# Behind the convolution in halves, and the last block of the pooling mixer split first

## What the reference computes

```python
def conformer_conv(h, w1, b1, w_dw, b_dw, ln_g, ln_b, w2, b2):      # mixer of layer 0
    u = h @ w1 + b1
    a, gate = split(u, 2)
    u = a * sigmoid(gate)
    u = depthwise causal conv of width 31 over the tokens + b_dw
    u = silu(layernorm(u, ln_g, ln_b))
    return u @ w2 + b2

def pool_mixer(h, w_grp, b_grp, scale):                             # mixer of layer 1
    for 4 groups of 256 features, windows 2, 4, 8, 16:
        p[g] = trailing mean of h[g] over the window - h[g]
    return (p[g] @ w_grp[g] + b_grp[g]) * scale

def sqrelu_mlp(h, w1, w2):                                          # behind either mixer
    return relu(h @ w1) ** 2 @ w2                                   # 1024 -> 4096 -> 1024
```

## Time and profile before

| | |
|---|---|
| time, median of 3 runs (lowest to highest) | 902.92 us (902.45 to 903.51) |
| the profiled execution: time | 903.05 us |
| its span, first to last instruction | 901.1 us |
| mean granted clock of TensorE | 0.997 of full |
| TensorE busy | 881.5 us, 98% of the span |
| VectorE busy | 704.9 us, 78% |
| ScalarE busy | 458.6 us, 51% |
| GpSimd busy | 149.1 us, 17% |

### The profile page before, as it was taken

One profiled execution on the slowest core, in us unless ns is written; L12 is line 12 of the kernel. 1 busy time (PEld: TensorE's weight loads), 2 busy tenths in 40 slices (PEclk: granted clock), 3 DMA queues, 4 the chain that ended last, 5 costly groups with the idle time before them and its releaser, 6 DMA issues.

```text
span 901.1 us, 11943 instructions
## 1 busy us (share of the span) xinstructions
PE 881.5 (98%) x4408; PEld 746.4 (83%) x4408; DVE 704.9 (78%) x946; ACT 458.6 (51%) x663; POOL 149.1 (17%) x128
## 2 busy tenths in 40 slices
PE   8999998999999999999999999999999999999996
PEld 8888876889888888888888888988888888888885
DVE  5799999867877778696868888687776868686856
ACT  5778686245462727354353645446262634435243
POOL 1499993270000020000000041000000000000000
PEclk9999999999999999999999999999999999999999
DMA  9614022205133131414224023113313142332102
GB/s 278 196 48 117 5 90 117 109 32 187 49 140 140 47 140 47 141 72 159 100 87 163 18 101 117 47 48 141 140 47 140 47 147 83 143 117 70 71 1 94
DMA packets 48376, 90.81 MB, mean 101 GB/s; under 512 B 1458, under 2 KB 18866, under 8 KB 48340
## 3 DMA queue, kind: packets, MB, share of 16 engines
q1 hardware_dynamic: 48340, 90.32, 29.2%
HBM read 88.22 MB, written 2.10 MB: 100 GB/s over the span
## 4 chain that ended last, share of the span: by engine, by line
PE 77%; DVE 8%; POOL 8%; DMA 2%; issue 2%; ACT 1%; SPq 0%; POOLq 0%; DVEq 0%; ACTq 0%
PE ps L1319 16%; PE ps L1321 16%; PE ps L1320 16%; PE ps L1520 10%; PE ps L1518 10%; PE ps L1519 10%; POOL w_lo L376 3%; POOL merged_a L386 3%; DMA w_raw<-in_conv_w 2%; POOL merged_b L386 2%; DVE ps L906 2%; PE ps L1338 1%; DVE tok L819 1%; DVE act_lo L825 1%; DVE bn L875 1%
## 5 line engine op out<-in xcount | busy, mean ns | idle before, releaser
L1319 PE MATMUL ps<-act_hi,w_hi 128*128 128x512 f32 (+1 forms) x712 | 262.2, 368 | 1.5 <-DVE act_lo L825 1.4
L1321 PE MATMUL ps<-act_hi,w_lo 128*128 128x512 f32 (+1 forms) x712 | 261.0, 367 | 0.0
L1320 PE MATMUL ps<-act_lo,w_hi 128*128 128x512 f32 (+1 forms) x712 | 261.0, 367 | 0.0
L1319 PEld LDWEIGHTS ps<-act_hi,w_hi 128*128 128x128 f32 x712 | 134.2, 189 | 23.8 <-DVE act_lo L825 2.0
L1520 PE MATMUL ps<-w_hi,u_lo 128*128 128x512 f32 x392 | 152.7, 390 | 0.0
L1518 PE MATMUL ps<-w_hi,u_hi 128*128 128x512 f32 x392 | 152.7, 389 | 0.0
L1321 PEld LDWEIGHTS ps<-act_hi,w_lo 128*128 128x128 f32 x712 | 134.2, 189 | 22.1
L1519 PE MATMUL ps<-w_lo,u_hi 128*128 128x512 f32 x392 | 152.5, 389 | 0.0
L1320 PEld LDWEIGHTS ps<-act_lo,w_hi 128*128 128x128 f32 x712 | 134.3, 189 | 21.8
L619 ACT ACTIVATE relu<-ps 128x512 f32<-128x512 f32 x36 | 21.5, 597 | 243.0 <-PE ps L1321 243.0
L1057 DVE TENSOR_TENSOR w_lo<-w_raw,w_hi 128x1024 fp32r<-128x1024 f32 x70 | 85.1, 1221 | 58.0 <-ACT w_hi L640 58.0
(11 more groups left out here) (206 smaller groups left out, 1274.8 us busy)
## 6 DMA issues: line engine op xcount, KB each, us to landing
w_raw<-in_mlp_w SPq DMA_DIRECT2D x32, 1024.0 KB, 5.0
w_raw<-in_mlp_w SPq DMA_DIRECT2D x16, 2048.0 KB, 8.1
w_raw<-in_conv_w SPq DMA_DIRECT2D x16, 512.0 KB, 5.9
w_raw<-in_conv_w SPq DMA_DIRECT2D x2, 2048.0 KB, 9.7
h<-in_x SPq DMA_DIRECT2D x4, 512.0 KB, 6.8
out<-tok SPq DMA_DIRECT2D x8, 256.0 KB, 2.3
gain<-in_norm_mix SPq DMA_DIRECT2D x2, 512.0 KB, 6.5
gain<-in_norm_mlp SPq DMA_DIRECT2D x2, 512.0 KB, 6.3
```

The lines of the kernel that those rows point to most:

```text
L1319: nc.tensor.matmul(dst, lh, rh, start=(n == 0), stop=False)
L1320: nc.tensor.matmul(dst, lh, rl, start=False, stop=False)
L1321: return nc.tensor.matmul(dst, ll, rh, start=False, stop=(n == count - 1))
```

## The change

Five parts:

1. In the last chunk of the convolution ScalarE takes 13 taps instead of 11, GpSimd 4 instead of 5, VectorE 14 instead of 15.
2. The statistics of the last chunk are read from PSUM bank 5; ScalarE copies it to `ctok` behind that read (`bn_read`).
3. Blocks 0 and 1 go through the norm in halves (with `center_half`, and half of block 2's), and the orders on VectorE and ScalarE are written anew; the four `c2b_low` stand behind the work on the blocks.
4. On TensorE the products of the rounded block (`out_high`) come ahead of those with the rest (`out_low`); each part waits for its half alone. 24 matmuls keep the clock instead of 28.
5. Pooling mixer: `proj_low(3)` stands ahead of `add_pool(2)`; `pool_band(3)` goes to banks 2 and 3 and does not wait for `add_pool(2)`; `add_pool(3)` stands behind `mlp_norm(2)`. The first MLP group of layer 1 uses banks 0, 1, 2, 3, starts with the rounded blocks, and turns blocks 2 and 3 behind j = 1 and j = 2.

```diff
-SHARE = (5, 5, 5, 5, 5, 5, 5, 11)
-POOL_LAST = 5
+SHARE = (5, 5, 5, 5, 5, 5, 5, 13)
+POOL_LAST = 4
...
 UP_BANK = (2, 3, 0, 1)
+FIRST_BANK = (UP_BANK, (0, 1, 2, 3))
...
         def pool_bank(b):
-            return 4 if b == 1 else 0
+            return (0, 4, 0, 2)[b]
...
             c2_high(3)
             nc.scalar.activation(stats[:, 3, 36:37], ident[:, 0:1], ACT.Sqrt)
+            act.wait_ge(bn_read, 1)
             ctok_copy(NC - 1)
...
-            c2b_high(0)
-            for b in range(1, NB):
-                if b >= 2:
-                    act_high(GEN_LN, b - 1)
+            def high_half(b, k):
+                if k == 0:
+                    act.wait_ge(turned_half, b + 1)
+                else:
+                    act.wait_ge(turned, 4 * GEN_LN + b + 1)
+                cs = slice(k * NC // 2, (k + 1) * NC // 2)
+                nc.scalar.copy(act_hi[:, cs, b * P:(b + 1) * P],
+                               turn_banks(GEN_LN, b)[:, cs]).then_inc(act_hi_ok if k else act_half_hi, 1)
+
+            def swish_sigmoid(b):
                 act.wait_ge(y_ok, b + 1)
                 act.wait_ge(tok_ok, 4 * GEN_LN + b)
                 nc.scalar.activation(spare, tok[:, b % 2, :], ACT.Sigmoid).then_inc(swish_sig, 1)
-                c2b_high(b)
-            act_high(GEN_LN, NB - 1)
+
+            high_half(0, 0)
+            act.wait_ge(y_ok, 1)
+            nc.scalar.activation(spare[:, high], tok[:, 0, high], ACT.Sigmoid).then_inc(swish_sig, 1)
+            high_half(0, 1)
+            swish_sigmoid(1)
+            act.wait_ge(w1_in, 16)
+            c2b_high(0)
+            high_half(1, 0)
+            high_half(1, 1)
+            swish_sigmoid(2)
+            c2b_high(1)
+            c2b_high(2)
+            act_high(GEN_LN, 2)
+            swish_sigmoid(3)
+            c2b_high(3)
+            act_high(GEN_LN, 3)
 
             def w1_high(layer, g, j):
...
             bn_part(1, 4, 7)
-            last = bn_part(2, 7, 8)
-            link(last)
+            dve.wait_ge(conv_turned, NC)
+            for b in range(NB):
+                last = nc.vector.bn_stats(bn[:, b, 2, :], ps[:, 4 + (NC - 1) % 2, b * P:(b + 1) * P])
+            last.then_inc(bn_read, 1)
+            dve.wait_ge(bn_read, 1)
             for b in range(NB):
                 last = nc.vector.bn_aggr(moments[:, b, :], bn[:, b].rearrange("p a k -> p (a k)"))
             link(last)
...
+            def center_half(b, k):
+                at = slice(k * 512, (k + 1) * 512)
+                link(nc.vector.scalar_tensor_tensor(tok[:, b % 2, at], ctok[:, b, at], moments[:, b, 0:1], gain[:, 0, at],
+                                                    ALU.subtract, ALU.mult))
...
+            def shift_half(b, k):
+                nc.vector.scalar_tensor_tensor(tok[:, b % 2, at], tok[:, b % 2, at], rinv[:, 32 + b:33 + b], gain[:, 1, at],
+                                               ALU.mult, ALU.add).then_inc(y_ok if k else y_half, 1)
...
+            def low_half(k):
+                if k == 0:
+                    dve.wait_ge(act_half_hi, 1)
+                else:
+                    dve.wait_ge(act_hi_ok, 4 * GEN_LN + 1)
+                cs = slice(k * NC // 2, (k + 1) * NC // 2)
+                nc.vector.tensor_tensor(act_lo[:, cs, 0:P], turn_banks(GEN_LN, 0)[:, cs], act_hi[:, cs, 0:P].bitcast(F32),
+                                        ALU.subtract).then_inc(act_lo_ok if k else act_half_lo, 1)
...
-            center(0)
+            dve.wait_ge(ctok_ok, NC)
+            center_half(0, 0)
...
+            shift_half(0, 0)
+            center_half(0, 1)
+            swish_half(0, 0)
+            shift_half(0, 1)
+            center(1)
+            swish_half(0, 1)
+            low_half(0)
             shift(1)
-            center(2)
-            swish(1)
+            dve.wait_ge(turned, 4 * GEN_LN + 1)
+            center_half(2, 0)
+            low_half(1)
+            swish_half(1, 0)
+            swish_half(1, 1)
+            center_half(2, 1)
             shift(2)
-            c2b_low(0)
+            dve.wait_ge(act_half_hi, 2)
             act_low(GEN_LN, 1)
+            swish(2)
             center(3)
-            swish(2)
             shift(3)
-            c2b_low(1)
             act_low(GEN_LN, 2)
             swish(3)
+            c2b_low(0)
+            act_low(GEN_LN, 3)
+            c2b_low(1)
             c2b_low(2)
-            act_low(GEN_LN, 3)
             c2b_low(3)
...
+            proj_low(3)
             add_pool(2)
-            proj_low(3)
             act_low(GEN_MLP1, 0)
             act_low(GEN_MLP1, 1)
-            mlp_norm(2, lambda: add_pool(3))
+            mlp_norm(2)
+            add_pool(3)
             mlp_norm(3)
             act_low(GEN_MLP1, 2)
             act_low(GEN_MLP1, 3)
...
-            keep_clock_long(28, act_hi[:, 0, 0:P], act_hi[:, 1, :])
+            def out_high(b, cs):
+                for c in cs:
+                    if b == 0 and c % 2 == 0:
+                        pe.wait_ge(c2_lo_ok, c // 2 + 1)
+                    nc.tensor.matmul(ps[:, b, :], act_hi[:, c, block_cols(b)], c2_hi[0][:, c, :], start=(c == 0), stop=False)
+                    nc.tensor.matmul(ps[:, b, :], act_hi[:, c, block_cols(b)], c2_lo[0][:, c, :], start=False, stop=False)
+
+            def out_low(b, cs):
+                for c in cs:
+                    last = nc.tensor.matmul(ps[:, b, :], act_lo[:, c, block_cols(b)], c2_hi[0][:, c, :], start=False,
+                                            stop=(c == NC - 1))
+                if NC - 1 in cs:
+                    last.then_inc(y_done, 1)
...
+            lower, upper = range(NC // 2), range(NC // 2, NC)
+            keep_clock_long(24, act_hi[:, 0, 0:P], act_hi[:, 1, :])
+            half_turn(0, 0)
+            pe.wait_ge(act_half_hi, 1)
+            out_high(0, lower[:3])
+            half_turn(0, 1)
+            out_high(0, lower[3:])
+            pe.wait_ge(act_half_lo, 1)
+            out_low(0, lower)
+            pe.wait_ge(act_hi_ok, 4 * GEN_LN + 1)
+            out_high(0, upper)
+            half_turn(1, 0)
+            pe.wait_ge(act_lo_ok, 4 * GEN_LN + 1)
+            out_low(0, upper)
+            half_turn(1, 1)
+            pe.wait_ge(act_half_hi, 2)
+            out_high(1, lower)
+            pe.wait_ge(act_hi_ok, 4 * GEN_LN + 2)
+            out_high(1, upper)
+            turn(GEN_LN, 2, tok[:, 0, :])
+            pe.wait_ge(act_lo_ok, 4 * GEN_LN + 2)
+            out_low(1, range(NC))
+            pe.wait_ge(act_hi_ok, 4 * GEN_LN + 3)
+            out_high(2, range(NC))
+            turn(GEN_LN, 3, tok[:, 1, :])
+            pe.wait_ge(act_lo_ok, 4 * GEN_LN + 3)
+            out_low(2, range(NC))
+            pe.wait_ge(act_hi_ok, 4 * GEN_LN + 4)
+            out_high(3, range(NC))
+            pe.wait_ge(act_lo_ok, 4 * GEN_LN + 4)
+            out_low(3, range(NC))
             pe.wait_ge(c2b_lo_ok, 4)
             for b in range(NB):
                 conv_out(b, 1, 4 + b, NC // 4, (lambda k=b - 2: turn(GEN_MLP0, k, tok[:, k % 2, :])) if b >= 2 else None)
...
-                    pe.wait_ge(act_lo_ok, 4 * gen + 2 * pair + 2)
+                    if pair or not layer:
+                        pe.wait_ge(act_lo_ok, 4 * gen + 2 * pair + 2)
                     for j in range(GF):
+                        bank = FIRST_BANK[layer][j]
                         if pair == 0:
                             pe.wait_ge(w1_lo_ok, 32 * layer + j + 1)
-                        if layer and pair == 0 and UP_BANK[j] == 0:
-                            pe.wait_ge(y_added, Y_POOL + NB)
+                        if layer and pair == 0 and j % 2 == 0:
+                            pe.wait_ge(y_added, Y_POOL + NB - 1 + j // 2)
+                        if layer and pair == 0 and j == 0:
+                            pe.wait_ge(act_hi_ok, 4 * gen + 2)
+                            for c in range(NC):
+                                nc.tensor.matmul(ps[:, bank, cols], m1_hi[:, 0, c, :], act_hi[:, c, cols], start=(c == 0),
+                                                 stop=False)
+                                nc.tensor.matmul(ps[:, bank, cols], m1_lo[:, 0, c, :], act_hi[:, c, cols], start=False,
+                                                 stop=False)
+                            pe.wait_ge(act_lo_ok, 4 * gen + 2)
+                            for c in range(NC):
+                                nc.tensor.matmul(ps[:, bank, cols], m1_hi[:, 0, c, :], act_lo[:, c, cols], start=False,
+                                                 stop=(c == NC - 1))
+                            continue
                         for c in range(NC):
-                            last = product(ps[:, UP_BANK[j], cols], (m1_hi[:, j, c, :], m1_lo[:, j, c, :]), act_tile(c, cols), c, NC)
+                            last = product(ps[:, bank, cols], (m1_hi[:, j, c, :], m1_lo[:, j, c, :]), act_tile(c, cols), c, NC)
                         if pair:
```

(6 more changed lines are left out.)

62 lines of the change are left out of this document (19 added, 43 removed).

## The result

The changed kernel takes 896.65 us (median of 5 runs, 896.41 to 896.84) beside 902.49 for the kernel before on the same chip (5 runs, 902.24 to 903.51): ratio 0.9934, 95% interval 0.9923 to 0.9944. The forecast was 898.1 with a range from 896.9 to 900.6. The direction was right; the time is 0.25 us under the low end. The profiled executions are 903.05 us (span 901.1) before and 896.41 us (span 894.6) after.

What follows compares the result with a forecast made beforehand. TensorE bounds the MLPs; elsewhere it waits for VectorE at the convolution's and pooling mixer's ends. Profiled 903.05 less 3.2 (convolution) and 1.65 (pooling) gives 898.2, or 898.1 us on the median's scale; range 896.9 to 900.6.

Steps and rivals of the forecast that it cites:

- The one tap: Convolution's end: one tap fewer on VectorE takes out 0.67 us, last tap ending at 139.93 instead of 140.60.
- the first shift: Convolution's end, VectorE: it starts at 145.11 instead of 146.39 us, by 0.67 for the tap and 0.61 for centring.
- statistics from PSUM: Convolution's last chunk: reading them from PSUM takes the same 0.90 us, and the moved copy comes out even.
- the first product: Start of `conv_out` on TensorE: at 148.6 instead of 151.17 us, 2.5 us earlier.
- the stretch to the second half: TensorE's first half of `conv_out` ends at 174.1 instead of 177.4 us, a gain of 3.2 us.
- the splits on VectorE: The four `c2b_low`, moved behind the work on block 3, end at 172.4 us, as before (172.53).
- last matmul: Where the pooling part's gain is read: 1.65 us from the pooling mixer's end, kept to the end.
- The centring alone: Convolution's end, VectorE: centring only half of block 0 ahead of the reciprocals saves 0.61 us.
- the sum's last line: Profiled 903.05 us less 3.2 and 1.65 gives 898.2, or 898.1 on the median's scale, 0.13 lower.
- the changed kernel's chopped stretch: Rival at `conv_out`'s half blocks: TensorE's clock falls once, costing 2.0 us, 900.1; chance 0.14, shared with late VectorE.
- That a part pays nothing: Two rivals: pooling mixer's gain lost, 899.7 us, chance 0.08; convolution's gain lost, 901.3 us, chance 0.04.
- The rival by which the clock stays at half through the half blocks: Convolution's end: slower than before if over 9.7 us run at half clock, up to 904.1 us; chance 0.04.

Runs made afterwards that it cites:

- the table's two pairs: Traces with and without a low clock ahead of 134 us, gated product to last matmul: kernel before 766.11 beside 766.10, changed kernel 761.07 beside 761.06.
- the second group's: The changed kernel run once more, unchanged, beside the kernel before: 896.51 and 902.62 us.
- filling the gap: Kernel before plus ten products into an unused bank where TensorE stood still ahead of the last transposes: 901.37 us, ratio 0.9990.
- the two parts alone: Kernel before with only the convolution's end changed, 898.55 us (0.9954), and with only the pooling mixer's end changed, 900.48 us (0.9976).
- the variant above: Changed kernel without its 24 products that keep the clock: 898.91 us, ratio 0.9962 to the kernel before.
- the 24 products: Kernel before with 24 products that keep the clock instead of 28: 901.37 us, ratio 0.9992.

## Why the prediction was a little off

**Held, with their sizes.** The one tap (0.67; without it 0.67 later), the first shift (1.28 predicted, 1.14 in the pair of traces once 1.53 is taken off), statistics from PSUM (no gain, no cost), the first product (2.5 predicted, 2.32), the stretch to the second half (3.2 predicted, 3.24), TensorE without a stall behind it, the splits on VectorE (172.4 predicted; 171.0, or 172.5 with 1.53 added back). The pooling mixer, less the 4.77 from ahead: band product 1.11 (1.13 predicted), MLP start 1.39 (1.40), last matmul 1.81 (6.58 less 4.77) against 1.65. The centring alone was mis-sized, 0.46 by its undoing where I had 0.61; where the pooling part's 0.16 more arises, behind the MLP's start, was not traced. The statement of the fixed term in the Trainium skill, "VectorE: DVE Perf Modes", section on the TRN2 errata, agrees here too: two halves of the shift take 2 × 0.75 us against 1.28 for a whole, or 1.41 back to back.

**The step that failed** is the sum's last line, "903.05 − 3.2 − 1.65 = 898.2 us on the profiled execution, which stands 0.13 above the median". It scales the time by 0.13 us, as if the execution in the profile were made up like the median one. It was not: it had the latest opening of all that were profiled, and it lost its clock at 130 to 134 us, where TensorE's work is hidden (the table's two pairs); its transposes ran late, and the gap ahead of VectorE's last tap was short. By its total it looked like the median. The three other profiled executions with its shares and that gap open 1.3 to 1.5 us earlier, stand still for 2.8 us there and lose the clock, which costs them 0.2 to 1.8 us (first product at 23.99, 24.33 and 25.54 us, against 23.74 and 23.75 with the clock kept). A term was missing, put at nothing: the clock that the change gives back, by the two taps that shorten the gap and by four products fewer ahead of the turn. The medians leave 5.84 − 5.05 = 0.8 us for it, or 1.1 with the second group's (902.62 less 896.51); filling the gap gave 0.96. The two agree, though the interval of 0.1 to 1.7 us is too wide to call the size settled, and the fall at the end of the pooling mixer may have a share in it. That 902.49 − 4.85 − 0.96 comes to 896.7, so near the measured 896.65, is in part luck. The row for it could be had: the earlier trace rows show the clock falling behind 2.1 us without work, and I read them only as a danger to the changed kernel, not as a loss that the kernel before might have in other executions and that two more taps of transposes would end. The change's own terms came to 5.05 us where I had 4.85; that by itself would have left the time inside the range.

**The rivals.** The clock did not fall in the changed kernel's chopped stretch. But the rival was near: each variant with a wait of 1.30 us or more there lost it, and is 1.9 to 6.9 us longer to the last matmul than the changed kernel, waits included. That a part pays nothing is refuted by the two parts alone. The rival by which the clock stays at half through the half blocks is refuted in the trace: with no products to keep it, in the variant above, it was back by 154 us, under 8 us behind the start of the first half turn (146.12). On the rule of the Trainium skill, "TensorE: Matmul & The Clock Gate", Part 4 on the PE-mode transpose, by which transposes don't count as busy in the same way: the kernel before with the new shares does nothing but transposes from 133.7 to 139.5 us, with one wait of 0.91, and its clock stays at 1.00, so this case doesn't bear it out.

**Open.** How many executions of the kernel before lose the clock ahead of block 0's turn is not known, as only profiled ones show the place: of four with its shares and nothing in the gap (the two of before, the pooling part, the 24 products), three did. The mean granted clock is on record for all. Of 79 executions of the kernel before in the four groups, 6 have 0.993, as the one profiled second, and take 903.35 to 903.89 us, so that one shows an uncommon and heavy case; 17 have 0.998, as the profiled one with the gap filled, with a median of 901.88; the 56 between them may have lost some in one of the places named here, with or without a cost. The pooling part's 2.1 against 1.8 us lies within the medians' uncertainty. Why the weights land 1.5 us later in some executions was not tried.

## What to carry to other kernels

Read a second execution of the kernel before you take a sum from one: a late opening can hide a loss that other executions have, with about the same total. To compare traces, measure between two marks that leave out what varies by itself, here the landing of the first weights and the last output. Where an edit opens or closes a gap of TensorE of a microsecond or two, cost it twice, once for its time and once for the clock; cheap products into an unused bank are the test and often the cure. Undoing one of the edits that close a gap can cost more than its own term: 1.9 us for a centring of 0.5.

## What the runs showed of the hardware

TensorE's clock fell behind gaps of 2.80, 2.49 and 2.00 us, and once with waits of 1.30 and 0.68 in a row; with 0.82 and 0.68 in a row it stayed, and so it did behind gaps of 1.48 and 1.64. With waits of 0.59 and 1.17 us at the end of the pooling mixer it fell in one trace and stayed in five, and behind a gap of 1.74 us ahead of the last chunk's transposes it fell in the changed kernel's second trace (128.32) and stayed with the gap filled later on (127.66). So here the length of a gap did not decide by itself. At half clock a 128x512 product starts every 0.43 us instead of 0.23, and four transposes take 1.11 us instead of 0.66. VectorE's short instruction took 2.18 us instead of 0.17 beside GpSimd's subtractions, and ended with them. In the kernel before, a two-input one on 128 x 1 elements took 1.72 us beside GpSimd's addition that ended at 528.76. The Trainium skill, "SBUF — State Buffer", section "Who interferes with whom", has VectorE and GpSimd lock each other out for a whole instruction in such forms; the traces agree. Statistics of four 128x128 tiles took 0.87 us from PSUM and 0.87 from SBUF (the changed kernel, and the kernel before in its second profile). Executions of one program differ by 1.3 us in the opening (127.43 and 126.09 at the gated product). Behind the last matmul they take 8.6 to 9.7 us more, the longer ones with VectorE waiting for the output's DMA.
